# Unread products ahead of the first transposes, and the queries of both token halves ahead of the keys in layer one

## The reference

```python
def first_block(x, p, positions, ...):
    h = x
    for i in range(DEPTH):
        a = rms_norm(h, attn_norm[i])
        proj = a @ w_in[i]
        (da_q, da_k, da_v, ssd_z, ssd_xbc, ssd_dt,
         gla_q, gla_k, gla_v, gla_g, gla_lr) = jnp.split(proj, IN_SPLITS, axis=-1)
        y_da = diff_attention(da_q, da_k, da_v, positions, ...)   # rms_norm and rotation of q and k first
        y_ssd = ssd_mixer(ssd_z, ssd_xbc, ssd_dt, ...)            # a 4-tap convolution over xbc first
        y_gla = gla_mixer(gla_q, gla_k, gla_v, gla_g, gla_lr, ...)
        h = h + jnp.concatenate([y_da, y_ssd, y_gla], axis=-1) @ w_out[i]
        ...                                                       # feed-forward, gate
    return h
```

## Time and profile before

| | us |
|---|---|
| median of 3 runs | 1627.56 (1627.25 to 1628.53) |
| the profiled execution | 1627.86 |
| its span, first to last instruction | 1626.0 |
| PE busy | 1605.7 (99%) |
| DVE busy | 906.1 (56%) |
| ACT busy | 192.5 (12%) |
| POOL busy | 54.8 (3%) |
| first product of q | starts 9.22 |
| layer one up to the products of `v` | up to 113.98 |

### The profile page before, as it was taken

The page is one execution under the profiler, slowest core; times in us unless marked ns, Lnnn a source line. Parts: engine busy times, 40 slices in busy tenths (PEclk is TensorE's granted clock), DMA queues, the critical chain, the costliest instruction groups (busy, mean ns, idle before and its releaser), DMA issues.

```text
span 1626.0 us, 20046 instructions
## 1 busy us (share of the span) xinstructions
PE 1605.7 (99%) x8505; PEld 1039.6 (64%) x8505; DVE 906.1 (56%) x1560; ACT 192.5 (12%) x310; POOL 54.8 (3%) x89
## 2 busy tenths in 40 slices
PE   8999999999999999999999999999999999999998
PEld 3866499974458655999545867997544444444442
DVE  3896776774659876766647676974421312222122
ACT  1321000000114110000002430500100000000000
POOL 1001030000010010000000000000000000000000
PEclk9999999999999999999999999999999999999999
DMA  5532564552633335454535333446899999999994
GB/s 195 207 111 104 168 172 156 160 203 103 209 139 127 140 109 165 156 176 158 205 131 180 123 110 105 161 157 270 369 427 427 428 427 427 427 428 426 428 427 176
DMA packets 116851, 374.66 MB, mean 230 GB/s; under 512 B 9956, under 2 KB 57672, under 8 KB 104728
## 3 DMA queue, kind: packets, MB, share of 16 engines
q1 hardware_dynamic: 113056, 370.36, 59.8%
q0 software_dynamic: 1232, 2.22, 0.7%
q10 hardware_dynamic: 2472, 0.77, 0.2%
HBM read 372.28 MB, written 1.05 MB: 230 GB/s over the span
## 4 chain that ended last, share of the span: by engine, by line
PE 96%; DVE 2%; DMA 1%; ACTq 0%; issue 0%; POOL 0%; SPq 0%; DVEq 0%; ACT 0%
PE bank L767 16%; PE bank L1060 15%; PE bank L1460 14%; PE bank L698 8%; PE bank L1512 7%; PE bank L710 6%; PE bank L1313 4%; PE bank L1437 3%; PE bank L1466 3%; PE bank L1263 3%; PE bank L1185 2%; PE bank L1043 2%; PE bank L1195 2%; PE bank L1346 2%; PE bank L718 1%; DMA weights<-in_w_in 1%
## 5 line engine op out<-in xcount | busy, mean ns | idle before, releaser
L1460 PE MATMUL bank<-arena,mix 128*64 128x512 f32 x608 | 188.1, 592 | 0.0
L698 PE MATMUL bank<-weights,turned_rows 128*128 128x512 f32 x384 | 169.8, 599 | 1.2 <-DMA weights<-in_w_in 0.7
L767 PE MATMUL bank<-arena 128*128 128x512 f32 x296 | 133.2, 592 | 0.0
L2955 DVE TENSOR_TENSOR mix<-mix,bank 128x512 f32<-128x512 f32 x16 | 16.8, 1052 | 204.9 <-PE bank L1460 204.9
L698 PEld LDWEIGHTS bank<-weights,turned_rows 128*128 128x128 f32 x384 | 72.7, 192 | 88.1 <-issue 86.0
L1460 PEld LDWEIGHTS bank<-arena,mix 128*64 128x64 f32 x608 | 60.3, 137 | 99.9 <-issue 99.9
L1460 PE MATMUL bank<-weights,mix 128*64 128x512 f32 x336 | 112.6, 592 | 0.0
L1060 PE MATMUL bank<-arena 128*128 128x128 f32 x960 | 110.5, 275 | 0.0
L1060 PEld LDWEIGHTS bank<-arena 128*128 128x128 f32 x960 | 108.8, 192 | 0.0
L767 PEld LDWEIGHTS bank<-arena 128*128 128x128 f32 x296 | 56.0, 190 | 69.9 <-issue 67.9
L710 PE MATMUL bank<-turned_rows,weights 128*128 128x256 f32 x448 | 98.6, 380 | 0.0
(11 more groups left out here) (515 smaller groups left out, 2395.9 us busy)
## 6 DMA issues: line engine op xcount, KB each, us to landing
weights<-in_w_in SPq DMA_DIRECT2D x29, 2048.0 KB, 8.1
arena<-in_w_up SPq DMA_DIRECT2D x22, 2048.0 KB, 19.1
arena<-in_w_gate SPq DMA_DIRECT2D x16, 2048.0 KB, 20.9
weights<-in_w_gate SPq DMA_DIRECT2D x16, 2048.0 KB, 16.9
arena<-in_w_down SPq DMA_DIRECT2D x15, 2048.0 KB, 22.4
weights<-in_w_ffn_gate SPq DMA_DIRECT2D x22, 1024.0 KB, 5.4
weights<-in_w_ffn_up SPq DMA_DIRECT2D x22, 1024.0 KB, 7.9
weights<-in_w_ffn_down SPq DMA_DIRECT2D x10, 2048.0 KB, 7.9
```

The lines of the kernel that those rows point to most:

```text
L698: ins = mm(b[:, :], xT[:, k, t0 + P * t:t0 + P * t + P], w[:, k, :], start=(k == 0), stop=(k == KD - 1))
L767: ins = mm(b[:, :], lhs[:, j, :], rhs[:, j, :], start=(first and j == 0), stop=(last and j == pairs - 1))
L1460: ins = mm(moe_bank[bank][SL * e:SL * e + SL, :], xsE[:, k, SL * e:SL * e + SL], w[e][:, k, :], start=(k == 0), stop=(k == KD - 1), skip_g ...
```

## The change

In front of the first rows' transposes PE makes six products of 128x128 from two constant tables into the last bank; nobody reads them. In layer one PE's order becomes q of half 0, with the transposes of the second rows between its blocks 3 and 4, q of half 1, k of half 0, the two parameter transposes, k of half 1, `lr`, `xbc0` part one, and only then `qk_turn(0)`. ACT copies q, q, k, then runs the two Sin activations, then copies the last k. Layer two keeps its order, and DVE, POOL and SP keep their lists. As chunk 3 is still issued at the end of q of half 1, it now is issued before k of half 0 is made.

```diff
+            for _ in range(6):
+                mm(psum[NPS - 1][:, 0:P], ident[:, :], tri[:, :], start=True, stop=True)
+
             def first_ahead(half):
 
+                if half:
+                    turn(TILE["n1", 0], xn, 1, "xn_ready")
                 half_turned(TILE["n1", 0], 0, half)
...
                 tokens_out(T("q"), ch, [0], ahead=first_ahead if layer == 0 else lambda half: half_turned(T("n1"), 0, half))
-                tokens_out(T("k"), ch + 1, [0], ahead=lambda half: turn(T("n1"), xn, 1, "xn_ready") if half else None)
+                if layer:
+                    tokens_out(T("k"), ch + 1, [0], ahead=lambda half: turn(T("n1"), xn, 1, "xn_ready") if half else None)
+                tokens_out(T("q"), ch, [1], ahead=lambda half: half_turned(T("n1"), 1, half))
                 if layer == 0:
+                    tokens_out(T("k"), ch + 1, [0])
                     pe.wait_ge(sem("rows_loaded"), 16 * 16)
...
-                tokens_out(T("q"), ch, [1], ahead=lambda half: half_turned(T("n1"), 1, half))
                 tokens_out(T("k"), ch + 1, [1])
...
-                qk_turn(0)
+                if layer:
+                    qk_turn(0)
                 channels_out(T("xbc0"), ch + 3, NM, SEQ, 2, range(2))
+                if layer == 0:
+                    qk_turn(0)
...
-                def copy_qk(t):
-                    for name, col in (("q", 0), ("k", 512)):
-                        copy(tm[:, t, col:col + 512], T(name) + t, psum[(T(name) + t) % NPS][:, :])
+                def copy_part(name, col, t):
+                    copy(tm[:, t, col:col + 512], T(name) + t, psum[(T(name) + t) % NPS][:, :])
...
-                copy_qk(0)
                 if layer == 0:
+                    copy_part("q", 0, 0)
+                    copy_part("q", 0, 1)
+                    copy_part("k", 512, 0)
                     act.wait_ge(sem("angle_ready"), n.next("angle_ready"))
                     act.activation(sin[:, :, :], ang[:, :, :], ACT.Sin).then_inc(sem("sin_done"), 1)
                     act.activation(cos[:, :, :], ang[:, :, :], ACT.Sin, scale=0.5).then_inc(sem("sin_done"), 1)
-                copy_qk(1)
+                    copy_part("k", 512, 1)
+                else:
+                    for t in range(NT):
+                        copy_part("q", 0, t)
+                        copy_part("k", 512, t)
```

## The result

| | before | changed |
|---|---|---|
| median of 15 runs each, us | 1628.02 (1626.65 to 1629.52) | 1631.00 (1629.02 to 1633.62) |
| profiled execution, us | 1627.86 | 1633.62 |
| its span, us | 1626.0 | 1631.9 |

The ratio is 1.0017, with an interval from 1.0010 to 1.0024: slower by 3 us, within the 0.2% that I had called no change. The forecast was 1628.9 and its range ended at 1631.3. The profiled execution is the slowest of the fifteen, so its own rows show more loss than the median does.

What follows compares the result with a forecast made beforehand. PE and DVE were taken to bound the kernel side by side up to `v`, 0.43 us apart. DVE's 1.74 us delay less that slack gave +1.31, hence 1628.9 us; PE's 1.36 gain became waiting. Range: 1626.8 to 1631.3.

Steps and rivals of the forecast that it cites:

- What bounds the kernel: PE and DVE run side by side up to `v`, 0.43 us apart; a delayed DVE start carries through undiminished.
- Six unread products: PE's start, before 7.24 us: the products take 3.0 us, end at 6.85 within idle time, and cost 0.
- What they may give: PE's start: an earlier clock rise could gain PE 0 to 2.6 us; taken as 0.
- Keys one product later: PE at 19.09 us: the wait for the keys' weights goes, as q of half 1 fills it; -0.71 us.
- `qk_turn(0)`, -0.65: PE at 42.69 us: its wait for DVE's finished queries and keys goes; -0.65 us for PE.
- What DVE pays: DVE's squares of q and k: the later copy of half 0's keys starts them 1.74 us later, at 33.97.
- What the loads pay: Parameter rows beside chunk 3: delayed 0 to 6.0 us; taken as 1.5, hidden, or 2.5 with an early clock rise.
- The sum: At `v`: DVE's 1.74 us less the 0.43 slack decides, +1.31 us; +2.1 with an early clock rise.
- rival 2: DMA engines, 24 to 34 us: loads collide, rows land over 3 us later; up to +5.6 us, 1633.1; chance 0.14.
- Rival 1: DVE's start does not move, given an early clock rise and undelayed rows; -0.43 us, 1627.1; chance 0.17.
- Rival 3: A DVE operation counted as rigid is paced by PE; time falls by 1.36 to 4.0 us; chance 0.08.
- The signs: Changed profile: PE's two waits gone, bank 7 copied near 33.3, L2026 near 34.0, new PE wait of 1 to 4 us.

Runs made afterwards that it cites:

- e1: The kernel before plus the six unread products alone, in the old order; 1628.81 us beside 1628.10, ratio 1.0008.
- e3: The changed kernel with chunk 3 issued when k of half 0 ends, not q of half 1; 1629.90 us, ratio 1.0010.
- e5: The changed kernel with DVE's angles waiting only for the positions and two gain rows, on their own semaphore; 1626.33 us, ratio 0.9992.
- e7: The changed kernel with nine more unread products ahead of layer one's wait for `gla_ready`; 1630.61 us, ratio 1.0018.
- e10: The kernel before with the six unread products and DVE's angles released early, as in e6; 1628.01 us, ratio 1.0002.
- e11: e5 with chunk 3 issued only at the end of k of half 0; 1627.69 us, ratio 0.9996.
- e12: e9 with a seventh unread product in front and one in PE's wait before the first product; 1626.70 us beside 1627.82, ratio 0.9994.
- e2: The changed kernel without the six unread products, so the new order alone; 1630.46 us, ratio 1.0013.
- e4: e3 without the six unread products; 1630.04 us, ratio 1.0009.
- e6: The kernel before with DVE's angles waiting only for the positions and two gain rows, on their own semaphore; 1627.52 us, ratio 0.9995.
- e8: e3 with nine more unread products ahead of layer one's wait for `gla_ready`; 1628.82 us, ratio 1.0004.
- e9: e5 with nine more unread products ahead of layer one's wait for `gla_ready`; 1628.30 us beside 1628.44, ratio 0.9998.

## Why the prediction came out as it did

- **What bounds the kernel** held: two chains side by side up to `v`, DVE's start carried through undiminished (+2.62 at L2041, +2.64 at L2246), slack 0.43. The table above bears that out over squares' starts from 31.4 to 35.3 us.
- **Six unread products, cost 0**: held where they stand. They end at 6.71, predicted 6.85, and the first transpose starts at 7.26 for 7.24.
- **What they may give**: I took 0 and should have taken 2.6 as the usual case. The clock rose between 7.0 and 9.0 us in eight of the nine profiles that had just the six products in front (changed, e1, e3, e5, e7 to e10), and at 13.38 in the ninth, e11. My reason for 0, the idle gap behind the unread work, does not stop the rise; by e11 and e12 it seems to make it unsure.
- **Keys one product later, -0.71, and `qk_turn(0)`, -0.65**: both waits went. PE reached the wait for `gla_ready` at 98.15 (100.53 less 2.38), with 2.4 us to spare for DVE. That is only 0.5 us earlier than before: 2.26 us of PE's gain had already gone in small waits for DVE from 56 to 75 us.
- **What DVE pays, +1.74 by the late keys**: this term was not the one that decided. The keys' copy stood at 30.96, 2.4 us earlier than the 33.33 of the text, because of the clock. e2 and e11 show the term where the clock is late: +0.96 and +1.44.
- **What the loads pay**: 2.62 us. The text took 2.5 with an early rise and 1.5 without; the first was the case and the size was right. The second was too much: in e2, with the late rise, the rows landed at 30.69, 0.2 later than before. The Trainium skill ("DMA: Bandwidth & Descriptors", Queues, rings and completion order) says that an engine takes turns between its queues, a packet at a time. The trace agrees in kind: the 16 KB loads became slower (7.0 us to landing beside chunk 3, 5.6 in e3 without it), but did not wait for the 12.1 us of chunk 3.
- **The sum, +1.31**: the rule gave +2.1 for the early rise, the traces give 2.62 - 0.43 = +2.19 of DVE, against a measured +2.98 between the medians. The forecast of 1628.9 took the wrong branch, 0.8 us too low, and two terms were missing from both. One is that the clock can fall again: in the profiled execution 1.3 us behind the new wait in layer one (117.50 less 116.17) and 1.6 us in the routing stage. The other is the 0.74 us at the end of the program. The 0.8 us between 2.19 and 2.98 leaves room for either, and the medians alone don't say how much each had. By my own shares +2.98 us lies outside the forecast's +0.5 to +2.6, in the place of rival 2, to which I gave 0.14. The range from 1626.8 to 1631.3 held it by 0.3 us, because it was drawn wide for the loads; that the unforeseen terms fitted in too is luck.
- **Rival 1** (DVE does not move, -0.43): refuted for the change; e3 is this rival made real at `v` (-0.25), though not in its median. **Rival 2** (the loads collide, slower): its place was right, its price not, 2.62 and not over 3. **Rival 3** (PE's gain comes through): refuted; PE waits for DVE.
- **The signs**: no DMA wait at 19 us, no wait at `qk_turn(0)`, a new wait at L874 of 2.38 us: right. Bank 7 near 33.3: wrong, 30.96. L2026 near 34.0: 34.85, later by the loads. PE shows new small waits for DVE from 56 to 75 us (1.22, 0.32, 0.41, 0.31), which I had not named and which belong to the same lateness.

What the median of e3 and e4 is made of takes one more look at the profiles. By `v` both should stand at or just below the kernel before, and both are 1.8 us or more above it, with no run below 1628.7. Behind `v` PE's list is the same in all kernels. Laid record by record beside that of the kernel before, it keeps one distance from 150 to 1160 us, to 0.02 us, and another from 1170 us to its end. Up to the last stores' issue nothing more changes by over 0.01 us; the rest of the span comes behind it. In us, against the kernel before:

| kernel | PE behind `v` | fall in the routing stage | behind PE's last record | span |
|---|---|---|---|---|
| changed | +3.51 | +1.61 | +0.75 | +5.87 |
| e2 | +0.69 | +1.61 | +0.01 | +2.31 |
| e3 | -0.19 | +1.60 | +0.75 | +2.16 |
| e4 | -0.09 | +1.64 | +0.74 | +2.29 |
| e5 | +0.30 | +1.59 | -0.42 | +1.47 |
| e7 | +2.75 | 0 | +0.74 | +3.49 |
| e12 | -0.82 | 0 | -0.42 | -1.24 |

The fall is in the profiles of the changed kernel, e2 to e6 and e8 and costs 1.6 us in each of the seven; those of before, e1, e7 and e9 to e12 don't have it. The end is +0.75 in the changed kernel, e1, e3, e4, e7 and e8, 0 in e2, and -0.42 in every kernel with early angles, e6 and e10 in the old order among them. So the profiled executions of e3 and e4 are explained to 0.01 us, and all that is left of their loss stands behind layer one.

Two questions stay open. Why the end differs between the kernels is not shown; its size splits them cleanly, but each has one profile. It counts against a part of what the early angles seem to give: 0.4 us against the kernel before, 1.2 against the changed one. And why the fall comes in most runs of e3, six of eleven by their mean clock of 0.996 or 0.997, is not shown either; no kernel was made that fills the waits of that stage. Nor does the fall explain all of e3's median: its four runs with 0.999 take 1628.71 to 1629.73 us, above the 1626.60 to 1628.10 of the nine such runs of the kernel before beside which it ran.

## What to carry to other kernels

When two engines run side by side with half a microsecond between them, work saved on one is worth next to nothing until the other's start is moved too. Here the new order with the unread products cost 3 us. Splitting one semaphore, so that VectorE waits only for the rows that it reads, took that loss away; that the order then gains anything over the old one is not shown. When an engine is made faster, look at what its results release: the early end of the queries sent 2 MB of weights out beside the small loads on which the second engine waits. And a wait of a few microseconds that is newly put into TensorE's list should be priced with its clock as well. Before a difference of 1 us is put down to an edit, the span should be split at the edited stage: what differs behind it, here a fall of the clock and the end of the program, may not be the edit's doing.

## What the runs showed of the hardware

- The clock fell to 0.50 after short waits: 2.38 us (changed) and 2.24 us (e5) ahead of `gla_ready`, 2.22 us in e10 for weights, and in the routing stage around waits of 0.68 and 0.93 us. It did not always fall there: 2.37 us in e3, 2.26 in e2, 2.27 in e11 and the 2.55 us wait for weights in e1 left it at 1.00, and the kernel before has the routing stage's waits (0.67 and 0.93 us) without a fall. Each fall in the routing stage cost 1.6 us, in seven profiles.
- With six unread products in front of the transposes the clock rose at 7.0 to 9.0 us in eight of nine profiles, without them at 10.8 to 13.3 us in four (before, e2, e4, e6).
- The same start can have its clock rise 5 us apart (7.8 in e9, 13.4 in e11, whose lists of PE are the same up to there), worth 2.2 us at `v`. The two groups of e9's runs, 2 us apart without a fall, fit this, and a profile of one execution shows one draw of it.
- A 2 MB load that set out beside the last small parameter loads took 12.1 us to land, and those landed 2.6 us later (33.10 for 30.48).
- From the issue of the last four stores, the same in all kernels, to the end of the span it took 4.49 us in six profiles, 4.92 in two and 5.65 in six.
